# Recurrence of a hybrid block on Trainium2: the second head's inverse factors on the opposite partition half, and a new order of the level products

## The chip, the cores and the metric

The kernel runs on one core of a Trainium2 chip. The metric is the device time in microseconds; before the change the median of three runs is 2850.46 us. Engines are called PE (TensorE), DVE (VectorE), ACT (ScalarE), POOL (GpSimd) and SP (SyncE, which issues DMAs here).

## The reference

Two layers over 1024 tokens of width 1024. The first layer mixes with eight RWKV-7 heads of 64 beside eight heads of dilated attention, the second with a Fourier transform; each is followed by a convolved GLU. The change touches only the RWKV recurrence, run once forward and once reversed:

```python
def step(state, inp):
    r_t, w_t, k_t, v_t, kk_t, a_t = inp
    sk = jnp.einsum('bhij,bhj->bhi', state, kk_t)
    state = (state * w_t[:, :, None, :]
             - sk[..., :, None] * (kk_t * a_t)[:, :, None, :]
             + v_t[..., :, None] * k_t[:, :, None, :])
    y = jnp.einsum('bhij,bhj->bhi', state, r_t)
    return state, y
```

The kernel computes it by chunks of 64 tokens. Inside a chunk the feedback of `sk` on later tokens is a 64x64 strictly lower triangular matrix for each head; one plus it has to be inverted. Everything is fp32.

## The kernel before, in words

`recurrence` (L1343) takes the 1024 tokens as 8 pairs (`NPAIR`) of two chunks. `g` is the direction (0 forward, 1 reversed), `m` the pair, `c` the chunk in it, `f` one of four pairs of heads (`KU`), `hh` the head in it; a unit `u = hh * KU + f` is one of eight (`UN`). An SBUF tile has 128 partitions: head `hh` of a head pair lies on partitions `head(hh)`, and things that belong to chunk `c` lie on the half `side(c)`, the other half being `other(c)`. So a 64x64 matrix uses a quarter of PE's array: its rows by the half of the inputs, its columns by the half of the output. Each fp32 product of the code stands in the profile as two MATMUL records with two weight loads.

For one pair PE does, for both directions in turn: `turn` (transposes), `scores` (products of the factors, 64x128), `lower` (the triangular matrix the other way round), `values`, then five levels (`LEVELS` = 2, 4, 8, 16, 32) that build the inverse by doubling, then `solve`, `carry` and four `step`s, the only part that hands state from chunk to chunk.

A level i makes three products for each unit and chunk: x (`level_x`, L1553) multiplies the scores `xn` by the inverse so far (X1 or T); DVE copies the result under a mask into XL (L1807). Then t (L1572) multiplies the transposed inverse (U1 or U) by XL, and DVE copies it into T (L1813, L1815); and u (L1581) gives the transposed inverse again, which ACT copies into U (L1668, L1670). The last level has no t. X1 and U1 are the start of the inverse and of its transpose: DVE copies X1 from the `lower` product (L1790) and U1 from the scores (L1797), under a mask of neighbouring pairs.

PE's order in a level is x for g = 0 and 1, then t and u for g = 0, then t and u for g = 1 (L1633 to L1637). All factors for the next pair are made beside this: on DVE one piece (`beside`, L1871) after the X copies and one after the T copies of a level, in the order scan (L1839), centre (L1845, L1847), shift (L1852), alphas (L1860 to L1864), nbetas (L1869), each for g = 0 and 1; on ACT `f_rates` after level 0 and `f_exps` after levels 1 and 2; on POOL `f_products` and `f_outputs`. SP loads the data for the pair after that once these are done (L1465 to L1471). Every engine works its own list in order, with semaphores between them. PSUM has eight banks, four for each direction (`bank(g, k)`): x goes to bank 3, t to bank 0, u to bank 1.

The lines are written out by hand; no planner orders them. After `recurrence` a barrier ends the stage.

Of the kernel before, what the change touches and what calls it, by code (L numbers as in the profile page):

```python
# [14 lines left out]
P = 128  # L15
# [1327 lines left out]
def recurrence(nc, z_d, vr_d, lw_d, aa_d, kk_d, tab, consts, ff, ysum, low, mix_out, bon_d, gate_d, yb_d, factors):  # L1343
# [9 lines left out]
    with ExitStack() as ctx:  # L1353
# [31 lines left out]
        vec, K_A = consts["vec"], 5  # L1385
        pb = s.ps("pb", [P, 8, 512])

        def sems(name):
# [58 lines left out]

        def narrow(g, k, b):
            return bank(g, k)[:, 0:UN * HC].rearrange("p (u q b) -> p u q b", u=UN, b=b)

# [37 lines left out]
        def _(pe):  # L1488
# [18 lines left out]
            def scores(g, m):  # L1507
                t = st[m % 2][g]
                for part in range(2):
                    pe.wait_ge(tok_c[g], 5 * m + (2 if part == 0 else 5))  # L1510
                    for f in (2 * part, 2 * part + 1):
                        for c in range(2):
                            for hh in range(2):
                                four = t[head(hh), f, 0:2 * P].rearrange("p (n t) -> p n t", t=CH)
                                alpha_rho = four[:, 1:3, :] if c == 0 else four[:, 0::3, :]
                                at = ((f % 2) * 2 + c) * P
                                out = bank(g, 2 * part + hh)[:, at:at + P].rearrange("p (n t) -> p n t", t=CH)
                                ins = mm(out, t[head(hh), f, (2 + c) * P:(3 + c) * P], alpha_rho, start=True, stop=True)
                    ins.then_inc(q_done[g], 1)

            def lower(g, m):
                t = st[m % 2][g]
                pe.wait_ge(q_c[g], 4 * m + 2)
                for f in range(KU):
                    for c in range(2):
                        for hh in range(2):
                            nbeta = t[head(hh), f, 2 * P + CH + c * CH:2 * P + CH + (c + 1) * CH]
                            ins = mm(bank(g, hh)[side(c), f * CH:(f + 1) * CH], t[head(hh), f, (1 - c) * CH:(2 - c) * CH], nbeta,
                                     start=True, stop=True)
                ins.then_inc(l_done[g], 1)  # L1530

            def values(g, m):
                pe.wait_ge(q_c[g], 4 * m + 4)
                pe.wait_ge(tok_c[g], 5 * m + 5)
                for u in range(UN):
                    hh, f = divmod(u, KU)
                    for c in range(2):
                        ins = mm(bank(g, 2)[side(c), u * CH:(u + 1) * CH], xn[g][other(c), hh, 2 * f + c, 0:CH], wv[g][other(c), c, u, :],
                                 start=True, stop=True)
                ins.then_inc(mv_done[g], 1)  # L1540

            def level_x(g, m, i):
                b = LEVELS[i]
                src = X1[g] if i == 0 else T[g]
                if i == 0:
                    pe.wait_ge(x1_c[g], 2 * m + 2)
                else:
                    pe.wait_ge(t_c[g], 4 * m + i)
                for u in range(UN):
                    hh, f = divmod(u, KU)  # L1550
                    for c in range(2):
                        out = bank(g, 3)[side(c), u * HC:(u + 1) * HC].rearrange("p (q b) -> p q b", b=b)
                        ins = mm(out, xn[g][side(c), hh, 2 * f + c, 0:CH], cols1(src[side(c), u, :], b, 0), start=True, stop=True)  # L1553
                ins.then_inc(x_done[g], 1)

            def level_tu(g, m, i):
                b = LEVELS[i]
                old = U1[g] if i == 0 else U[g]
                if i == 0:
                    pe.wait_ge(u1_c[g], 2 * m + 2)  # L1560
                else:
                    pe.wait_ge(u_c[g], NL * m + i)
                pe.wait_ge(x_c[g], NL * m + i + 1)
                if i < NL - 1:
                    for u in range(UN):
                        for c in range(2):
                            if i == 0:
                                out, x = bank(g, 0)[side(c), u * CH:(u + 1) * CH], XL[i][g][side(c), u, :]
                            else:
                                out = bank(g, 0)[side(c), u * HC:(u + 1) * HC].rearrange("p (q b) -> p q b", b=b)  # L1570
                                x = cols1(XL[i][g][side(c), u, :], b, 0)
                            ins = mm(out, old[side(c), u, :], x, start=True, stop=True)  # L1572
                    ins.then_inc(t_done[g], 1)
                for u in range(UN):
                    for c in range(2):
                        if i == 0:
                            out, y = bank(g, 1)[side(c), u * CH:(u + 1) * CH], old[side(c), u, :]
                        else:
                            out = bank(g, 1)[side(c), u * HC:(u + 1) * HC].rearrange("p (q b) -> p q b", b=b)
                            y = cols1(old[side(c), u, :], b, 1)  # L1580
                        ins = mm(out, XL[i][g][side(c), u, :], y, start=True, stop=True)  # L1581
                ins.then_inc(u_done[g], 1)

            def solve(g, m):
                pe.wait_ge(u_c[g], NL * m + NL)
                pe.wait_ge(mv_c[g], m + 1)
                for u in range(UN):
                    hh, f = divmod(u, KU)
                    for c in range(2):
                        ins = mm(bank(g, 2 + hh)[side(c), f * P:(f + 1) * P], U[g][side(c), u, :], rz[g][side(c), u, :],  # L1590
                                 start=True, stop=True)
                ins.then_inc(z_done[g], 1)
# [53 lines left out]
        def _(act):  # L1646
# [13 lines left out]
            def values(g, m):  # L1660
                act.wait_ge(mv_done[g], m + 1)
                A(rz[g][:, :, CH:2 * CH], bank(g, 2).rearrange("p (u e) -> p u e", u=UN), ACT.Copy).then_inc(mv_c[g], 1)

            def level_u(g, m, i):
                b = LEVELS[i]
                act.wait_ge(u_done[g], NL * m + i + 1)
                if i == 0:
                    A(U[g][:, :, :], bank(g, 1).rearrange("p (u e) -> p u e", u=UN), ACT.Copy).then_inc(u_c[g], 1)  # L1668
                else:
# [38 lines left out]
            for m in range(NPAIR):  # L1708
# [3 lines left out]
                for i in range(NL):  # L1712
                    for g in range(2):
                        level_u(g, m, i)
                    if m + 1 < NPAIR:
                        if i == 0:
# [48 lines left out]
        def _(dve):  # L1765
# [19 lines left out]
            def lower(g, m):  # L1785
# [3 lines left out]
                for hh in range(2):  # L1789
                    V.copy_predicated(X1[g][:, hh * KU:(hh + 1) * KU, :], pairs[:, 0:1, :].broadcast_to([P, KU, CH]),  # L1790
                                      bank(g, hh)[:, 0:KU * CH].rearrange("p (f n) -> p f n", f=KU)).then_inc(x1_c[g], 1)

            def upper(g, m):
                dve.wait_ge(q_c[g], 4 * m + 4)
                for c in range(2):
                    mask = pairs[side(c), 1:2, :].rearrange("p (a b) n -> p a b n", a=1).broadcast_to([CH, 2, KU, CH])
                    V.copy_predicated(units(U1[g][side(c), :, :]), mask, xn[g][side(c), :, c::2, 0:CH]).then_inc(u1_c[g], 1)  # L1797

            def level_x(g, m, i):
# [6 lines left out]
                mask = level[:, i, :].rearrange("p (u q b) -> p u q b", u=1, b=b).broadcast_to([P, UN, HC // b, b])  # L1806
                V.copy_predicated(cols(XL[i][g][:, :, :], b, 0), mask, narrow(g, 3, b)).then_inc(x_c[g], 1)  # L1807

            def level_t(g, m, i):
                b = LEVELS[i]  # L1810
                dve.wait_ge(t_done[g], (NL - 1) * m + i + 1)
                if i == 0:
                    V.tensor_copy(T[g][:, :, :], bank(g, 0).rearrange("p (u e) -> p u e", u=UN)).then_inc(t_c[g], 1)  # L1813
                else:
# [39 lines left out]
            def f_alphas(g, m):  # L1854
# [35 lines left out]
            for m in range(NPAIR):  # L1890
                beside(m, 0)
                for phase in (scores, lower, upper):
                    for g in range(2):
                        phase(g, m)
                for i in range(NL):
                    for g in range(2):
                        level_x(g, m, i)
                    beside(m, 2 * i + 1)
                    if i < NL - 1:
                        for g in range(2):  # L1900
                            level_t(g, m, i)
                        beside(m, 2 * i + 2)
                for g in range(2):
# [1691 lines left out]
```

## Time and profile before

| | |
|---|---|
| median of three runs | 2850.46 us (2849.05 to 2860.39) |
| profiled execution, span from first to last instruction | 2846.2 us |
| profiled execution, what lies around the span | the page gives no number |
| recurrence | from the first transposes at about 671 us to the last product at 1122.8 us |
| one pair | 54.1 to 56.5 us |
| busy in the second pair (54.14 us) | PE 51.0, DVE 31.7, ACT 22.1, POOL 11.3 us |

PE's matmuls are pipelined: a row of the time line shows from the start of its first record to the end of its last, and the next row may start before that end. The pace of a block is therefore read from start to start.

### The profile page before, as it was taken

How to read it: one execution, taken by the hardware profiler on the slowest of the kernel's cores; microseconds unless marked ns; L12 is line 12 of the kernel's file. 1: busy time of each engine (PE TensorE's matmuls, PEld its weight loads, DVE VectorE, ACT ScalarE, POOL GpSimd, SP SyncE). 2: the span in 40 equal slices, each digit the busy share in tenths (PEclk: the TensorE clock that was granted, in tenths of full speed). 3: DMA queues.
4: the chain of work that ended last, by engine and by line, in shares of the span. 5: the costliest groups of instructions: out<-in, count | busy, mean ns of one | idle time of the engine just before them, and what ended most of it. 6: DMA issues, size and time to landing. Idle time of an engine off the chain costs nothing. (4 is left out here: it accounts for less than half of the span.)

```text
span 2846.2 us, 54939 instructions
## 1 busy us (share of the span) xinstructions
PE 2625.7 (92%) x23187; PEld 2149.5 (76%) x23187; DVE 1603.8 (56%) x2296; ACT 1138.0 (40%) x1802; POOL 918.1 (32%) x625
## 2 busy tenths in 40 slices
PE   5998998896999999979999999997897999999998
PEld 5776556576989888758888888875776888888887
DVE  7775532457555544666555564455655555556445
ACT  4211342553344333344444444454434444444434
POOL 2302121104112210225877770000412777773000
PEclk9999999898999999989999999997998999999999
DMA  6676434602311220422222228543122222225654
GB/s 232 229 270 215 168 133 175 186 17 64 92 48 48 71 91 27 133 80 69 89 83 77 86 90 284 169 164 109 52 92 71 89 89 74 82 89 216 191 181 145
DMA packets 295928, 346.48 MB, mean 122 GB/s; under 512 B 28384, under 2 KB 224213, under 8 KB 295685
## 3 DMA queue, kind: packets, MB, share of 16 engines
q1 hardware_dynamic: 286044, 336.64, 36.6%
q10 hardware_dynamic: 9640, 6.33, 0.7%
q8 instruction: 185, 3.03, 0.4%
q14 instruction: 59, 0.48, 0.1%
HBM read 271.58 MB, written 71.34 MB: 120 GB/s over the span
## 5 line engine op out<-in xcount | busy, mean ns | idle before, releaser
L2847 POOL TENSOR_TENSOR cg_u_lo<-cg_u_raw,cg_u_hi 128x512 fp32r<-128x512 f32 x210 | 315.2, 1509 | 146.8 <-ACT cg_u_hi L2733 146.8
L131 PE MATMUL cg_ps<-m_hi,cg_u_hi 128*128 128x512 f32 x844 | 331.2, 392 | 26.0 <-DVE cg_u_lo L2922 21.7
L133 PE MATMUL cg_ps<-m_hi,cg_u_lo 128*128 128x512 f32 x844 | 330.0, 391 | 0.0
L132 PE MATMUL cg_ps<-m_lo,cg_u_hi 128*128 128x512 f32 x808 | 315.5, 390 | 0.0
L2733 ACT ACTIVATE cg_u_hi<-cg_u_raw 128x512 fp32r<-128x512 f32 x216 | 132.1, 629 | 380.5 <-PE cg_ps L133 229.8
L131 PEld LDWEIGHTS cg_ps<-m_hi,cg_u_hi 128*128 128x128 f32 x844 | 159.7, 189 | 61.1 <-DVE cg_u_lo L2922 22.5
L131 PE MATMUL cg_ps<-over_y_tx,cg_u_hi 128*128 128x512 f32 x480 | 186.7, 389 | 0.0
L132 PE MATMUL cg_ps<-over_y_tx,cg_u_hi 128*128 128x512 f32 x480 | 186.7, 389 | 0.0
L133 PE MATMUL cg_ps<-over_y_tx,cg_u_lo 128*128 128x512 f32 x480 | 186.7, 389 | 0.0
L133 PEld LDWEIGHTS cg_ps<-m_hi,cg_u_lo 128*128 128x128 f32 x844 | 159.5, 189 | 33.5
L2899 DVE SCALAR_TENSOR_TENSOR cg_z<-cg_ps,top_conv_f,cg_z 128x1023 f32<-128x1023 f32 x88 | 113.0, 1284 | 115.1 <-ACT cg_z L2757 115.1
L132 PEld LDWEIGHTS cg_ps<-m_lo,cg_u_hi 128*128 128x128 f32 x808 | 152.7, 189 | 31.8
L2847 POOL TENSOR_TENSOR cg_u_lo<-cg_u_s,cg_u_hi 128x512 fp32r<-128x512 f32 x80 | 103.7, 1296 | 63.5 <-ACT cg_u_hi L2733 63.5
L1745 POOL TENSOR_TENSOR rw_kd<-rw_kd,att_kx 128x512 f32<-128x512 f32 x16 | 24.7, 1543 | 280.1 <-ACT rw_kd L1690 280.1
L2902 DVE SCALAR_TENSOR_TENSOR cg_z<-cg_ps,top_conv_f,cg_z 128x1023 f32<-128x1023 f32 x88 | 112.9, 1283 | 3.1
L131 PE MATMUL za_ps<-h_hi,za_w_hi 128*128 128x512 f32 x256 | 103.7, 405 | 8.2 <-POOL za_w_lo L1029 8.2
L2757 ACT ACTIVATE cg_z<-cg_ps,top_conv_f 128x1024 f32<-128x1024 f32 x88 | 98.1, 1115 | 21.0 <-DVE cg_ps L2959 11.6
L132 PEld LDWEIGHTS cg_ps<-over_y_tx,cg_u_hi 128*128 128x128 f32 x480 | 90.1, 188 | 18.7
L133 PEld LDWEIGHTS cg_ps<-over_y_tx,cg_u_lo 128*128 128x128 f32 x480 | 90.1, 188 | 18.7
L131 PEld LDWEIGHTS cg_ps<-over_y_tx,cg_u_hi 128*128 128x128 f32 x480 | 90.1, 188 | 18.7
L131 PE MATMUL cg_ps<-over_f_d_hi,cg_a_hi 128*128 128x512 f32 x248 | 97.4, 393 | 6.3 <-DVE cg_a_lo L2918 6.3
L132 PE MATMUL za_ps<-h_lo,za_w_hi 128*128 128x512 f32 x256 | 100.9, 394 | 0.0
(475 smaller groups left out, 6515.2 us busy)
## 6 DMA issues: line engine op xcount, KB each, us to landing
cg_u_raw<-in_ffn_up SPq DMA_DIRECT2D x88, 512.0 KB, 5.1
cg_u_raw<-in_ffn_down SPq DMA_DIRECT2D x64, 512.0 KB, 4.7
qkv_mw<-in_ada_w SPq DMA_DIRECT2D x12, 2048.0 KB
over_f_d_raw<-in_ffn_down SPq DMA_DIRECT2D x48, 512.0 KB, 5.2
scr_act<-cg_z SPq DMA_DIRECT2D x44, 512.0 KB, 2.7
qkv_mw<-in_ada_w SPq DMA_DIRECT2D x8, 1024.0 KB, 11.4
next_w<-in_mix_in SPq DMA_DIRECT2D x16, 512.0 KB, 6.6
za_out<-in_ada_w SPq DMA_DIRECT2D x8, 1024.0 KB
```

Source lines behind the costliest of these rows:

```text
L131: nc.tensor.matmul(out, a_hi, b_hi, start=first, stop=False)
L132: nc.tensor.matmul(out, a_hi, b_lo, start=False, stop=False)
L133: return nc.tensor.matmul(out, a_lo, b_hi, start=False, stop=last)
L1745: TT_(kd[g][:, :, :], kd[g][:, :, :], kx[g][:, :, :], ALU.mult).then_inc(f_kd[g], 1)
L2733: A(u_hi[:, n % RING], source(g, i), ACT.Copy).then_inc(uhi_done, 1)
L2757: A(z[:, x, :], both(g, x), ACT.Copy, scale=conv_cols[:, 1, g + x * FT:g + x * FT + 1]).then_inc(mid_done, 1)
L2847: G.tensor_tensor(u_lo[:, n % RING], source(g, i), u_hi[:, n % RING].bitcast(F32), ALU.subtract).then_inc(ulo_done, 1)
L2899: V.scalar_tensor_tensor(z[:, x, 1:S], both(g, x)[:, 0:S - 1], conv_cols[:, 0, c:c + 1], z[:, x, 1:S], ALU.mult, ALU.add).then_inc(left_do ...
L2902: V.scalar_tensor_tensor(z[:, x, 0:S - 1], both(g, x)[:, 1:S], conv_cols[:, 2, c:c + 1], z[:, x, 0:S - 1], ALU.mult, ALU.add).then_inc(con ...
```

## The change

1. For the second head (`u >= KU`) the start of the inverse and all that follows lie on `home(c, u) = other(c)`. `lower` writes the second head's U1 product as well, by 8 more products for each direction (16 records), and DVE copies that part of U1 from PSUM (one more copy for each direction), the first head's part still from the scores (64x256 instead of 64x512).
2. The factor alpha is stored with its halves in another order for the second head, so its write on DVE becomes two writes of 64 partitions each.
3. Products and copies of `values`, x, t, u and `solve` take `home(c, u)` for the second head. x, t, `values` and `solve` go over f, then hh, then c. Results of a level are spread over two banks: x and t in banks 0 and 1, u in banks 2 and 3, at 128 columns a unit.
4. Order of the levels on PE: x(0) for both directions, then for each level and direction t, u and directly behind them the x of the next level of the same direction. On DVE: T copy, one `beside` piece, next X copy, for each direction. On ACT `f_rates` and `f_exps` follow the U copy of their own direction, in levels 0 and 1.

The core of the diff:

```diff
-        def alpha_of(g, m):
-            a = halves(st[m % 2][g][:, :, 0:P])
-            return a[:, :, ::-1, :] if g == 0 else a[:, :, :, ::-1]
+        def alpha_of(g, m, hh):
+            a = halves(st[m % 2][g][head(hh), :, 0:P])
+            a = a if g == 0 else a[:, :, :, ::-1]
+            return a[:, :, ::-1, :] if g == hh else a
+        def alpha_slot(c, hh):
+            return slice(((1 - c) ^ hh) * CH, (((1 - c) ^ hh) + 1) * CH)
+        def home(c, u):
+            return side(c) if u < KU else other(c)
+        def wide(g, r):
+            return pw[:, (2 * g + r) * UN:(2 * g + r + 1) * UN, :]
@@ PE, lower
+                for f in range(KU):
+                    for c in range(2):
+                        nbeta = t[head(1), f, 2 * P + CH + c * CH:2 * P + CH + (c + 1) * CH]
+                        ins = mm(bank(g, 1)[other(c), (KU + f) * CH:(KU + f + 1) * CH], nbeta, t[head(1), f, alpha_slot(c, 1)],
+                                 start=True, stop=True)
@@ PE, level_x
-                for u in range(UN):
-                    hh, f = divmod(u, KU)
-                    for c in range(2):
-                        out = bank(g, 3)[side(c), u * HC:(u + 1) * HC].rearrange("p (q b) -> p q b", b=b)
-                        ins = mm(out, xn[g][side(c), hh, 2 * f + c, 0:CH], cols1(src[side(c), u, :], b, 0), start=True, stop=True)
+                for f in range(KU):
+                    for hh in range(2):
+                        u = hh * KU + f
+                        for c in range(2):
+                            out = wide(g, 0)[home(c, u), u, 0:HC].rearrange("p (q b) -> p q b", b=b)
+                            ins = mm(out, xn[g][side(c), hh, 2 * f + c, 0:CH], cols1(src[side(c), u, :], b, 0), start=True, stop=True)
@@ PE, level_tu: t (the same loops over f, hh, c), then u (still over u, c)
+                                    out = wide(g, 0)[side(c), u, 0:HC].rearrange("p (q b) -> p q b", b=b)
+                                    x = cols1(XL[i][g][home(c, u), u, :], b, 0)
+                                ins = mm(out, old[home(c, u), u, :], x, start=True, stop=True)
...
+                            out = wide(g, 1)[home(c, u), u, 0:HC].rearrange("p (q b) -> p q b", b=b)
+                            y = cols1(old[home(c, u), u, :], b, 1)
+                        ins = mm(out, XL[i][g][home(c, u), u, :], y, start=True, stop=True)
@@ PE, solve (the same loops over f, hh, c)
+                            ins = mm(bank(g, 2 + hh)[side(c), f * P:(f + 1) * P], U[g][home(c, u), u, :], rz[g][home(c, u), u, :],
+                                     start=True, stop=True)
@@ PE, order
+                for g in range(2):
+                    level_x(g, m, 0)
                 for i in range(NL):
                     for g in range(2):
-                        level_x(g, m, i)
-                    for g in range(2):
                         level_tu(g, m, i)
+                        if i + 1 < NL:
+                            level_x(g, m, i + 1)
@@ ACT, order
                 for i in range(NL):
                     for g in range(2):
                         level_u(g, m, i)
-                    if m + 1 < NPAIR:
-                        if i == 0:
-                            for g in range(2):
+                        if m + 1 < NPAIR:
+                            if i == 0:
                                 f_rates(g, m + 1)
-                        elif i <= 2:
-                            f_exps(i - 1, m + 1)
+                            elif i == 1:
+                                f_exps(g, m + 1)
@@ DVE, lower, upper, f_alphas
+                V.copy_predicated(U1[g][:, KU:UN, :], pairs[:, 1:2, :].broadcast_to([P, KU, CH]),
+                                  bank(g, 1)[:, KU * CH:UN * CH].rearrange("p (f n) -> p f n", f=KU)).then_inc(x1_c[g], 1)
...
-                    V.copy_predicated(units(U1[g][side(c), :, :]), mask, xn[g][side(c), :, c::2, 0:CH]).then_inc(u1_c[g], 1)
+                    V.copy_predicated(U1[g][side(c), 0:KU, :], pairs[side(c), 1:2, :].broadcast_to([CH, KU, CH]),
+                                      xn[g][side(c), 0, c::2, 0:CH]).then_inc(u1_c[g], 1)
...
-                V.tensor_tensor(alpha_of(g, m), halves(kk[g][:, :, :]), halves(lw[g][:, :, :]), ALU.mult).then_inc(f_alpha[g], 1)
+                V.tensor_tensor(alpha_of(g, m, 0), halves(kk[g][head(0), :, :]), halves(lw[g][head(0), :, :]), ALU.mult)
+                V.tensor_tensor(alpha_of(g, m, 1), halves(kk[g][head(1), :, :]), halves(lw[g][head(1), :, :]), ALU.mult).then_inc(f_alpha[g], 1)
@@ DVE, order
-                for i in range(NL):
+                for g in range(2):
+                    level_x(g, m, 0)
+                beside(m, 1)
+                for i in range(NL - 1):
                     for g in range(2):
-                        level_x(g, m, i)
-                    beside(m, 2 * i + 1)
-                    if i < NL - 1:
-                        for g in range(2):
-                            level_t(g, m, i)
-                        beside(m, 2 * i + 2)
+                        level_t(g, m, i)
+                        beside(m, 2 * i + 2 + g)
+                        level_x(g, m, i + 1)
```

## Rows read from the trace of the kernel before

**Rows 1.** The page, part 1: busy time, share of the span and instructions of each engine.

```profile
PE 2625.7 (92%) x23187; PEld 2149.5 (76%) x23187; DVE 1603.8 (56%) x2296; ACT 1138.0 (40%) x1802; POOL 918.1 (32%) x625
```

**Rows 2.** Windows, two chunk pairs: stretch, length, busy of five engines (instructions), clock, DMA, GB/s.

```profile
730.86:785.00 54.14, 51.01 (x1509) 49.56 (x1505) 31.72 (x60) 22.11 (x48) 11.27 (x8) 1.00 0.23 62
...
840.34:896.80 56.46, 52.66 (x1509) 51.21 (x1505) 31.57 (x60) 22.11 (x48) 11.25 (x8) 0.97 0.22 59
```

**Rows 3.** Time line of PE, second pair: start, duration, operation, records, [idle before].

```profile
739.44 0.69 PE L1528 MATMUL rw_pb<-lt_low 64*64 64x64 f32 x32 [0.48 <-DVE rw_xn L1781]
739.96 1.87 PE L1538 MATMUL rw_pb<-rw_wv,rw_xn 64*64 64x64 f32 x58
...
745.72 1.15 PE L1572 MATMUL rw_pb<-rw_XL,rw_U 64*64 64x64 f32 x32 [2.05 <-DVE rw_XL L1807]
746.67 1.13 PE L1581 MATMUL rw_pb<-rw_U,rw_XL 64*64 64x64 f32 x32
747.61 1.13 PE L1572 MATMUL rw_pb<-rw_XL,rw_U 64*64 64x64 f32 x32
...
749.47 2.04 PE L1553 MATMUL rw_pb<-rw_T,rw_xn 64*64 64x32 f32 x64
...
769.98 3.39 PE L1590 MATMUL rw_pb<-rw_rz,rw_U 64*64 64x128 f32 x58
...
773.49 2.00 PE L1599 MATMUL rw_pb<-rw_xn,rw_zt 64*64 64x128 f32 x60
776.08 0.69 PE L1612 MATMUL rw_pb<-rw_wv,rw_xn 128*64 128x64 f32 x16 [0.59 <-DVE rw_rg L1822]
```

**Rows 4.** Groups by line, DVE, fifth pair: count, busy us, mean ns, idle before.

```profile
L1807 DVE COPY_PREDICATED rw_XL<-rw_level,rw_pb 128x256 f32<-128x256 uint32 x10 | 4.8, 498 | 4.3 <-PE rw_pb L1553 4.3
L1797 DVE COPY_PREDICATED rw_U<-rw_pairs,rw_xn 64x512 f32<-64x512 uint32 x4 | 2.9, 731 | 0.1
L1815 DVE COPY rw_T<-rw_pb 128x256 f32<-128x256 f32 x6 | 2.5, 418 | 1.7 <-PE rw_pb L1572 1.6
L1839 DVE TENSOR_TENSOR_SCAN rw_cc<-rw_reset_row,att_lw 128x512 f32<-128x512 f32 x2 | 2.4, 1196 | 0.0
L1847 DVE TENSOR_TENSOR rw_cc<-rw_cc,rw_mids 128x512 f32<-128x512 f32 x2 | 2.3, 1168 | 0.1
L1852 DVE TENSOR_TENSOR att_lw<-rw_cc,att_lw 128x512 f32<-128x512 f32 x2 | 1.5, 772 | 0.0
...
L1790 DVE COPY_PREDICATED rw_X<-rw_pairs,rw_pb 128x256 f32<-128x256 uint32 x4 | 1.4, 436 | 0.0
L1862 DVE COPY rw_ends<-rw_e 128x4 f32<-128x4 f32 x2 | 1.4, 696 | 0.0
...
L1864 DVE TENSOR_TENSOR lt_low<-att_kk,att_lw 128x512 f32<-128x512 f32 x2 | 1.4, 678 | 0.0
```

**Rows 5.** Time line of DVE, second pair.

```profile
744.88 1.28 DVE L1807 COPY_PREDICATED rw_XL<-rw_level,rw_pb 128x256 f32<-128x256 uint32 x2
...
752.09 1.65 DVE L1847 TENSOR_TENSOR rw_cc<-rw_cc,rw_mids 128x512 f32<-128x512 f32 x1
```

**Rows 6.** Time line of ACT, second pair.

```profile
771.99 0.60 ACT L1675 ACTIVATE rw_zt<-rw_pb 128x512 f32<-128x512 f32 x1 [1.39 <-PE rw_pb L1590]
```

**Rows 7.** Windows, PE alone: stretch, length, busy (records), granted clock, DMA share, GB/s.

```profile
687.50:692.50 5.00, 3.84 (x79) 0.67 0.02 3
...
911.67:914.85 3.18, 3.18 (x64) 0.55 0.00 0
1023.50:1028.50 5.00, 4.40 (x103) 0.66 0.01 3
...
775.00:777.50 2.50, 1.91 (x62) 1.00 1.08 271
```

**Rows 8.** Time line of SP's queue, second pair: issue of the loads.

```profile
766.64 0.36 SPq L1471 DMA_DIRECT2D att_lw<-scr_lw  x1
```

**Rows 9.** Windows, PE alone, as rows 7: end of the loads' traffic.

```profile
777.50:780.00 2.50, 2.49 (x73) 1.00 0.71 197
```

More of the change, by code:

```diff
@@ L1514, in scores @@
                                 four = t[head(hh), f, 0:2 * P].rearrange("p (n t) -> p n t", t=CH)
-                                alpha_rho = four[:, 1:3, :] if c == 0 else four[:, 0::3, :]
+                                alpha_rho = (four[:, 1 - hh:3:1 + hh, :] if c == 0 else four[:, hh::3 - hh, :])
                                 at = ((f % 2) * 2 + c) * P
@@ L1534, in values @@
                 pe.wait_ge(tok_c[g], 5 * m + 5)
-                for u in range(UN):
-                    hh, f = divmod(u, KU)
-                    for c in range(2):
-                        ins = mm(bank(g, 2)[side(c), u * CH:(u + 1) * CH], xn[g][other(c), hh, 2 * f + c, 0:CH], wv[g][other(c), c, u, :],
-                                 start=True, stop=True)
+                for f in range(KU):
+                    for hh in range(2):
+                        u = hh * KU + f
+                        for c in range(2):
+                            ins = mm(bank(g, 2 + hh)[home(c, u), f * CH:(f + 1) * CH], xn[g][other(c), hh, 2 * f + c, 0:CH],
+                                     wv[g][other(c), c, u, :], start=True, stop=True)
                 ins.then_inc(mv_done[g], 1)
@@ L1564, in level_tu @@
                 if i < NL - 1:
-                    for u in range(UN):
-                        for c in range(2):
-                            if i == 0:
[L1568 to L1572, printed above, removed]
+                    for f in range(KU):
+                        for hh in range(2):
+                            u = hh * KU + f
+                            for c in range(2):
+                                if i == 0:
+                                    out, x = wide(g, 0)[side(c), u, 0:CH], XL[i][g][home(c, u), u, :]
+                                else:
+                                    out = wide(g, 0)[side(c), u, 0:HC].rearrange("p (q b) -> p q b", b=b)
+                                    x = cols1(XL[i][g][home(c, u), u, :], b, 0)
+                                ins = mm(out, old[home(c, u), u, :], x, start=True, stop=True)
                     ins.then_inc(t_done[g], 1)
@@ L1586, in solve @@
                 pe.wait_ge(mv_c[g], m + 1)
[L1587 to L1591, printed above, removed]
+                for f in range(KU):
+                    for hh in range(2):
+                        u = hh * KU + f
+                        for c in range(2):
+                            ins = mm(bank(g, 2 + hh)[side(c), f * P:(f + 1) * P], U[g][home(c, u), u, :], rz[g][home(c, u), u, :],
+                                     start=True, stop=True)
                 ins.then_inc(z_done[g], 1)
@@ L1661, in values @@
                 act.wait_ge(mv_done[g], m + 1)
[L1662 removed]
+                both_banks = pb[:, 4 * g + 2:4 * g + 4, 0:KU * CH].rearrange("p h (f e) -> p h f e", f=KU)
+                A(units(rz[g][:, :, CH:2 * CH]), both_banks, ACT.Copy).then_inc(mv_c[g], 1)
             def level_u(g, m, i):
@@ L1667, in level_u @@
                 if i == 0:
-                    A(U[g][:, :, :], bank(g, 1).rearrange("p (u e) -> p u e", u=UN), ACT.Copy).then_inc(u_c[g], 1)
+                    A(U[g][:, :, :], wide(g, 1)[:, :, 0:CH], ACT.Copy).then_inc(u_c[g], 1)
                 else:
```

29 lines of the change are left out of this document (14 added, 15 removed).

## The prediction

> **What bounds the kernel now.** Read first the busy line of the page: PE is busy 92% of the 2846.2 us span, the next engine, DVE, 56% [rows 1]. The page's chain of waits covers only the last quarter of the span, in other functions, so it says nothing of this stage; what a change here is worth must be read from the stage itself, which is one stretch of the time line: everything after it starts when its last product is out. The windows cut it into its eight chunk pairs, 54.1 to 56.5 us each [rows 2]. In the undisturbed second pair PE is busy 51.0 of 54.1 us, DVE 31.7, ACT 22.1, POOL 11.3. So PE bounds it, with one hole: before the first inverse product t0 it waits 2.05 us for DVE [rows 3]. I write x, t and u for the three products of a level and X, T, U for the copies that follow them on DVE, DVE and ACT.
>
> The time line of PE gives the price of a matmul record (one product of the code is two records). 64 records of x take 2.04 us of which the last one's tail is 0.2, 32 of t 0.95 from start to start (745.72 to 746.67), 32 of u 0.94: some 29 ns each, whether they stream 32 or 64 columns. They use two quarters of the array, since rows and output columns lie on the same half. `lower` already spreads over four quarters: 32 records from 739.44 to 739.96, 0.52 us or 16.3 ns each. With 128 columns, solve (two quarters) takes 3.5 us for 64 (769.98 to 773.49) and carry (four) 2.0 for 60, less a tail of 0.25, so 54 and 29 ns [rows 3].
>
> **The change on PE**, per pair, both directions. A block of 32 records going from two quarters to four falls from 0.93 to 0.52, by 0.41.
> - values: 2 blocks, -0.82. x: 10 blocks, -4.1. t: 8 blocks, -3.3. Solve: 3.5 to 1.9, -1.6.
> - u stays at 0.93: its rows and its output lie on the same half for either head.
> - `lower` gains 16 records a direction. They all read the second head's rows. Between 16.3 and 29.2 ns each that is 0.26 to 0.47; I take 0.47, +0.94, since they have only two quarters.
> - Scores, turn, carry and steps keep their counts.
> Together PE's work falls by 8.9 us a pair. That would be 71 us over eight pairs, if nothing else came late. DVE does.
>
> **Up to t0.** DVE sets this point today. After the scores it runs four X1 copies (0.44 each, 0.36 from start to start), four 64x512 U1 copies (0.73 each) [rows 4] and from 744.88 the first X (two of them 1.28, so 0.64) [rows 5]; then PE starts t0 at 745.72 [rows 3]. After the change: six copies of 0.36 instead of four (+0.72), and the U1 copies halve to 64x256. No row has that form; 0.73 of a form twice as long bounds it above and half of that, 0.37, below. I take 0.38, nearest to the 128x256 X1 copies at 0.36 each, so -1.4. The net is -0.7 a pair. The shorter values and x0 and the longer `lower` all lie before this point: the hole before t0 grows and they are worth nothing.
>
> **From t0 to solve**: today 745.72 to 769.98, 24.2 us without a hole [rows 3]. New PE work: t and x 8 blocks each at 0.52, u 10 at 0.93, together 17.6. Now the new order: for each direction t, u, and its next x directly behind them; on DVE T, one piece of the next pair's factors, then X. Half a level is 0.52+0.93+0.52 = 1.97 us of PE. DVE needs T 0.42 and X 0.44, from start to start 0.35 and 0.38, and the piece: centre 0.9 when alone (0.16 and 0.69) and up to 1.8 where it meets POOL (1.65 for its large part [rows 5], mean 1.17 [rows 4]), I take 1.4 for the second direction; shift 0.75; nbetas 0.65, like the product L1864 at 0.68; alphas that product and three small ones, one of which, a copy of 4 elements, has a mean of 0.70 where it meets POOL: 1.0 for the first direction and 1.8 for the second [rows 4]. The alphas are now two 64-partition writes: between 0 and another 0.6; I take 0.6, since the 64-partition form of 512 elements (0.73) is no cheaper than the 128-partition ones (0.68) [rows 4]. So:
> - The first T cannot start before the second X (0.64) and the scan (1.20) are through, and takes 0.62: some 2.5 us after the first X, where PE has work for 1.45. Hole 0.96.
> - The half level with the second direction's alphas: 0.35+2.4+0.38 = 3.13 against 1.97. Hole 1.16. The one before it (2.33) eats the slack, and centre (2.1 to 2.4) leaves 0.2 to 0.3 more; together some 0.35.
> Holes 2.5, stretch 20.1, saved 4.1. I followed the chain on the other side too: U must be copied before the same direction's next t, which is 2.5 us behind u, and ACT needs 0.2+0.38 plus at most one rates or exps piece of 1.6 to 1.8 before it. It just fits. POOL's pieces and the loads move with the factors: the loads for the next pair are issued from nbetas on (766.64) and their traffic lasts to about 780, 14 us [rows 8, 9]; the next scan starts some 17 us after nbetas, 3 us of cover (that cover gone, the scan and everything in DVE's queue behind it, the scores first, would be late).
>
> **From solve to the first step**: today 6.1 us (769.98 to 776.08). Solve and carry would be 1.9 and 1.9, but ACT is in between: a Z copy of 0.60 (771.99 [rows 6]), two wv copies of 0.6, then the other direction's Z copy; the second carry starts at about 3.7 instead of 4.4 and the first step, behind it on PE, at 4.65. Saved 1.4. Steps are as before.
>
> **Sum**: 0.7+4.1+1.4 = 6.2 us a pair for the seven pairs that carry factor work, 43.4; the last has none beside its levels, so no holes there: about 8.6. Total 52. From that I take 4: t and solve walk the halves in the order high, low, low, high, so neighbours share input rows, which `lower` and carry never do. Between 16.3 and 29.2 ns I take 19 for t, +0.8 of PE a pair, of which the holes hide some. Left: 48.
>
> One rule of the Trainium skill speaks against exactly this. "TensorE: Matmul & The Clock Gate", section "The mechanism" of its part on packing: a weight load overlaps matmuls in flight only when the row group differs. By it, t and solve would lose some of the gain; no row here has that order. The same page, "Wait — 56ns, not 53.3ns?", puts the least distance between matmul starts at about 25 ns. The 16.3 ns of `lower` contradicts it [rows 3]; by the page x and t would be 0.8 us a block and the time an estimated 2825.
>
> **Clock.** In four of eight pairs the granted clock fell from 2.4 to 1.2 GHz behind the hole before t0 (first and last row and the one at 911.67, with 3.18 us for what takes 1.87: 1.3 lost) [rows 7]. After the change the hole is longer (about 1.7, behind 0.8 in two parts), so I count a fall in all eight pairs. But t0 and u0 then run into the 0.96 in which PE would wait for T anyway, so each costs about 0.7: 5.6 against 5.2 today. Counted as nothing. A stretch that is 1.91 of 2.50 busy held 2.4 GHz [rows 7], and the levels will be about 85% busy.
>
> The profiled execution's span is 2846.2; 2846.2-48 = 2798, and the median of the runs lies 4.3 above the span, for what lies around it: **2803 us**.
>
> **Rivals.**
> 1. *Four quarters do not pay with these orders* (output in two banks, halves in another order; the change then does not do what it says). x, t, values, solve stay at 29 and 54 ns; what is left are the 0.7 before t0 and an equal loss in `lower` and the alphas. 2850, within 0.5%. For: no row has 64x32 on four quarters. Against: `lower` and carry hold 16 and 29 ns with either stride. Chance 0.08. In part (25 ns) it is 2825, inside the range.
> 2. *Slower: the clock stays at 1.2 GHz in the levels*, since they now have holes where today they have none. At 1.2 GHz a u block takes 1.73 instead of 0.93 (as t did at 911.67), x and t 0.96: half a level 3.65, the stretch about 32.7 against 20.1, +12.6. Against 6.2 gained, that is +6.4 a pair, 2901 if it always happens; it decides from about half of the stretch at the low clock. For: the falls at today's only hole. Against: 2.4 GHz at 76% busy. Chance 0.07.
> 3. *DVE holds less*: centre and alphas no longer meet POOL's writes (0.70 for a copy of 4 elements [rows 4], 1.65 for a centre of 0.69 [rows 5]), t at 16.3. Another 1.5 us a pair: 2791. Chance 0.15.
> 4. *DVE holds more*: pieces meet POOL in every half level, or PE stands more often for reasons that the profile does not name, as it does today in some pairs (the fourth is 2.3 us longer than the second [rows 2]). 2 us a pair: 2819. Chance 0.2.
> The forecast itself 0.5, its own range 2796 to 2810.
>
> 0.5% is 14 us, about what a measurement here can tell. Faster: forecast, rivals 3 and 4 and the partial case, 0.85; same 0.08; slower 0.07. The range goes from rival 3 to the partial case and a little of rival 1: 2788 to 2835.
>
> **What would show it.** Right: x and t blocks of 32 records at 0.5 to 0.6 us; u unchanged at 0.93; PE holes of about 1 us at x1 and x4, released by DVE's T; pairs of 47 to 49 us; solve to step 4.7. Wrong: blocks still at 0.9; t clearly slower than x; a granted clock of 0.5 inside the levels; a scan that waits for its load; PE waiting for ACT's U.

## The result, and the profile after

The changed kernel takes 2863.35 us (median of 20 runs, 2857.43 to 2869.55) against 2851.51 of before (20 runs). The ratio is 1.004, with a 95% interval of 1.0031 to 1.005: slower by 0.4%, where 1.7% faster was forecast. The profiled span is 2856.9 us against 2846.2.

The page's busy line of the changed kernel, beside [rows 1]:

```profile
PE 2610.3 (91%) x23443; PEld 2130.3 (75%) x23443; DVE 1627.2 (57%) x2328; ACT 1135.7 (40%) x1802; POOL 921.2 (32%) x625
```

PE has 15 us less to do and the span is 11 longer. The window of its second pair (stretch, length, busy of PE, PE's weight load, DVE, ACT and POOL with instructions, clock, DMA share, GB/s), beside [rows 2]:

```profile
732.80:790.20 57.40, 52.98 (x1541) 50.64 (x1537) 34.94 (x64) 21.85 (x48) 11.69 (x8) 0.79 0.21 59
```

57.4 us for 54.1, with a granted clock of 0.79 of full speed where it was 1.00. The time line of PE in the same pair, beside [rows 3]:

```profile
745.32 0.77 PE L1572 MATMUL rw_pb<-rw_X,rw_xn 64*64 64x32 f32 x36 [1.06 <-issue]
747.19 0.69 PE L1594 MATMUL rw_pb<-rw_XL,rw_U 64*64 64x64 f32 x32 [1.10 <-DVE rw_XL L1834]
747.67 1.61 PE L1603 MATMUL rw_pb<-rw_U,rw_XL 64*64 64x64 f32 x32
...
755.82 0.60 PE L1572 MATMUL rw_pb<-rw_T,rw_xn 64*64 64x32 f32 x28
...
756.29 0.65 PE L1594 MATMUL rw_pb<-rw_XL,rw_U 64*64 64x32 f32 x30
756.76 1.06 PE L1603 MATMUL rw_pb<-rw_U,rw_XL 64*64 64x32 f32 x30
...
764.59 1.08 PE L1572 MATMUL rw_pb<-rw_T,rw_xn 64*64 64x32 f32 x32 [0.55 <-DVE rw_T L1842]
765.46 1.06 PE L1594 MATMUL rw_pb<-rw_XL,rw_U 64*64 64x32 f32 x32
766.32 1.79 PE L1603 MATMUL rw_pb<-rw_U,rw_XL 64*64 64x32 f32 x30
...
775.70 3.46 PE L1613 MATMUL rw_pb<-rw_rz,rw_U 64*64 64x128 f32 x62
...
781.54 0.69 PE L1635 MATMUL rw_pb<-rw_wv,rw_xn 128*64 128x64 f32 x16 [0.34 <-DVE rw_rg L1849]
```

The reader is to see four things. The x block at 755.82 and the t block at 756.29 are 32 records each, a few of them in small rows that are left out here. With those, x goes from 755.74 to 756.23 and t from there to 756.76, where u follows: the four quarters do what was said, about 0.5 us a block. The u block is near the old 0.93 (756.76 to 757.69). But from 762 on the same blocks take twice as long: t from 765.46 to 766.32 is 0.86, and u from 766.32 on 1.5 and more. And solve starts 28.5 us after t0 (747.19 to 775.70), not 20.1 as forecast and not 24.2 as before. The windows of PE alone over the same stretch (busy with records, granted clock, DMA share, GB/s), beside [rows 7]:

```profile
747.19:755.00 7.81, 7.63 (x228) 0.56 0.02 4
755.00:762.00 7.00, 5.99 (x287) 0.98 0.02 7
762.00:775.70 13.70, 13.15 (x337) 0.50 0.48 138
775.70:781.50 5.80, 5.44 (x132) 0.73 0.53 136
```

The clock falls to 1.2 GHz behind the hole at t0, comes back near 755, and falls again at 762 behind a hole of 0.95 us in an x block (before 761.35, put down to "issue"). This time it stays down through all that is left of the levels, 13.7 us, although PE is 96% busy there (the wait of 0.55 before 764.59 lies inside this stretch). It comes back only in solve and carry. All eight pairs show such a long stretch, 10 to 17 us. Over the whole recurrence, before and then after:

```profile
680.00:1120.00 440.00, 407.79 (x11868) 0.98 0.20 58
```

```profile
680.00:1120.00 440.00, 386.00 (x11909) 0.84 0.21 60
```

A mean clock of 0.98 in 440 us is 18 us at 1.2 GHz, one of 0.84 is 141. And DVE meets POOL in new places; the alphas' two writes in this pair, where the kernel before has one write of 0.68 (L1864, [rows 4]):

```profile
761.39 0.67 DVE L1891 TENSOR_TENSOR rw_st<-att_kk,att_lw 64x512 f32<-64x512 f32 x1
762.08 1.67 DVE L1892 TENSOR_TENSOR rw_st<-att_kk,att_lw 64x512 f32<-64x512 f32 x1
```

### The profile page after: what moved, and what is told of

Its sections match the earlier page's. It is cut to its first block and busy times, and to the rows that moved or that the text cites. A ratio compares the mean times of both kernels' runs of the same rounds, so it can differ in the third digit from the quotient of the medians.

```text
span 2856.9 us, 55483 instructions
## 1 busy us (share of the span) xinstructions
PE 2610.3 (91%) x23443; PEld 2130.3 (75%) x23443; DVE 1627.2 (57%) x2328; ACT 1135.7 (40%) x1802; POOL 921.2 (32%) x625
## 5 line engine op out<-in xcount | busy, mean ns | idle before, releaser
L1603 PE MATMUL rw_pb<-rw_U,rw_XL 64*64 64x32 f32 (+1 forms) x2560 | 122.2, 258 | 4.7 <-issue 4.7
L1603 PEld LDWEIGHTS rw_pb<-rw_U,rw_XL 64*64 64x64 f32 x2560 | 115.6, 179 | 5.3 <-issue 5.3
```

The costliest lines, as they stand in the source:

```text
L1603: ins = mm(out, XL[i][g][home(c, u), u, :], y, start=True, stop=True)
```

## The experiments

Theory A when they began: the clock ate the gain; it falls behind holes of PE in the levels, and the 32-column blocks behind them do not bring it back. Its rivals were the order (B), holes alone with no part for the columns (C) and the four quarters themselves (D). The kernel before was run again in each set, with medians of 2848.27 to 2851.51; each ratio is taken to the one of its own set. A wait that the profile puts down to "issue" is one in which PE waited for nothing that the profile names.

**Taking the change apart.** The old order back in the changed kernel:

```diff
-                for g in range(2):
-                    level_x(g, m, 0)
                 for i in range(NL):
                     for g in range(2):
-                        level_tu(g, m, i)
-                        if i + 1 < NL:
-                            level_x(g, m, i + 1)
+                        level_x(g, m, i)
+                    for g in range(2):
+                        level_tu(g, m, i)
```

(the lists of ACT and DVE likewise)

> The changed kernel with the order of before (x of both directions, then t and u of each; DVE and ACT pieces where they were); halves and four quarters as changed. Theory A: the clock is what ate the gain. It falls behind a hole of PE in the levels and the 32-column blocks do not bring it back. PE is then as short of work as in the changed kernel, the holes are elsewhere, and the time stays near the changed kernel's: 2840 to 2870, with stretches at 1.2 GHz in most pairs. Rival B: the new order makes the holes, and four quarters alone would gain: 2800 to 2820, hardly a low clock in the levels.

Measured: 2857.97, ratio 1.0024 (1.0009 to 1.004); mean clock 0.84 in the recurrence, as in the changed kernel. B falls: it is not the order that loses the clock. The median is 5 us below the changed kernel's, with intervals that overlap, so a small price of the order is neither shown nor excluded.

The opposite, the new order alone in the kernel before (the three lists changed as in the diff of the change, no half moved):

> The kernel before with only the new order on PE, DVE and ACT; every product still on two quarters. Half a level is then 2.8 us of PE against at most 2.5 of DVE. Theory A: no holes in the levels, the clock holds, 2843 to 2855. Rival B (the order costs by itself): above 2860, with holes released by DVE's copies in the levels.

Measured: 2861.06, ratio 1.0036 (1.0019 to 1.0052), but its profiled execution is the shortest of the ten, 2847.84 (span 2846.1), with a clock of 0.99 in the recurrence. The median lies at the edge that B named and the profile where A expected it. The record has the mean clock of every execution over the whole kernel: 0.970 in the profiled one, 0.968 in the next shortest (2854.43), 0.958 to 0.963 in the other eight, 2857 to 2865. So part of the spread goes with the clock. It is not all: the kernel before has mostly 0.957 to 0.966 too, and a median 10 us lower. A cost of the order by itself, some 10 us here, stays open; the one profile does not show where it would lie.

**64 columns.** x, t and u stream all columns; the copies pick theirs:

```diff
-                            out = wide(g, 0)[home(c, u), u, 0:HC].rearrange("p (q b) -> p q b", b=b)
-                            ins = mm(out, xn[g][side(c), hh, 2 * f + c, 0:CH], cols1(src[side(c), u, :], b, 0), start=True, stop=True)
+                            out = wide(g, 0)[home(c, u), u, 0:CH]
+                            ins = mm(out, xn[g][side(c), hh, 2 * f + c, 0:CH], src[side(c), u, :], start=True, stop=True)
...
-            return wide(g, r)[:, :, 0:HC].rearrange("p u (q b) -> p u q b", b=b)
+            return cols(wide(g, r)[:, :, 0:CH], b, which)
```

> The changed kernel, but x, t and u stream all 64 columns in every level, and the copies pick the columns they need. The blocks are no longer at 2.4 GHz, since a record takes 16 and 29 ns with 32 and with 64 columns alike. Theory A says that the clock came back in before after 64-column blocks and does not after 32-column ones: here it falls as before in some places and comes back within 3 to 5 us, 2805 to 2835. Rival C: only holes matter, not columns: 2855 to 2870 as the changed kernel, low stretches of 15 us.

Measured: 2843.5, ratio 0.9965 (0.9951 to 0.9979), 20 us below the changed kernel for twice the columns. The mean clock is back to 0.95:

```profile
680.00:1120.00 440.00, 367.12 (x12276) 0.95 0.22 63
```

The low stretches in it last 3 to 7 us. C falls. The time is 8 us above A's range, though: the clock gave back 20 us, and something else holds.

**Less DVE work in the levels.**

```diff
+                k = KU if m < 2 else 1
-                V.tensor_tensor(lw[g][:, :, :], cc[g][:, :, :], lw[g][:, :, :], ALU.subtract).then_inc(f_before[g], 1)
+                V.tensor_tensor(lw[g][:, 0:k, :], cc[g][:, 0:k, :], lw[g][:, 0:k, :], ALU.subtract).then_inc(f_before[g], 1)
```

(alphas and nbetas likewise)

> The changed kernel with three quarters of DVE's shift, alphas and nbetas left out from the third pair on (it uses stale factors there). That takes away the hole at the alphas and leaves the one before t0. Theory A: with fewer holes the clock falls less often; levels from pair 3 on at 2.4 GHz past t0, 2800 to 2830. Rival D: the clock falls with 32-column blocks on four quarters whether there is a hole or not: 2850 or more.

Measured: 2859.36, ratio 1.0023 (1.0004 to 1.0041); mean clock 0.85. A's number fails. (This kernel leaves three quarters of the three pieces out from the third pair on and uses stale factors.) Seven of the eight pairs still lose the clock for 10 to 21 us. So the hole at the alphas is not needed: the clock also fell behind smaller ones, one of them behind a single "issue" wait of 0.98 us (fall at 883.1). The number is D's, but each of these falls has some wait of PE shortly before it, so D's "whether there is a hole or not" is not shown; no run has four quarters, 32 columns and no hole. The next two runs decide how far columns alone go.

**The same hole with 32 and with 64 columns, on two quarters.** In the kernel before, DVE gets extra work before the T copies of level 2 (`pad` is an unused tile, `padded` a new semaphore):

```diff
+                    if i == 2:
+                        for k in range(8):
+                            V.tensor_tensor(pad[:, :], reset_row[:, 0:416], reset_row[:, 0:416], ALU.mult).then_inc(padded, 1)
+                            dve.wait_ge(padded, m * 8 + k + 1)
```

> The kernel before with eight extra DVE operations (5 us) before the T copies of level 2, in every pair: a hole of PE of about 3 us in front of 32-column blocks on two quarters. The holes alone cost about 24 us: 2875. Theory A (32-column blocks do not bring the clock back): it falls in most pairs and stays at 1.2 GHz to the end of the levels, 12 us and more, 2900 to 2930. Rival C (the clock comes back after about 3 us whatever the blocks): 2875 to 2888.

> The same hole in the kernel before, but with 64 columns streamed in every level. Theory A: the clock falls as often and comes back within 3 to 5 us, 2875 to 2890, at least 15 below the run with the hole and 32 columns. Rival C: the same time as that run, within 5.

Measured: 2974.36 with 32 columns (four executions) and 2912.84 with 64 (three), ratios 1.0437 (1.0406 to 1.0468) and 1.0224 (1.0192 to 1.0255). A fourth execution with 64 took 7838.3 us; no run shows why, and it is left out. The holes came out as 6.8 us, not 3, so both lie higher than expected; the difference between them is some 61 us, 7.7 a pair. With 32 columns, the row behind the hole and windows of PE alone:

```profile
790.22 3.63 PE L1554 MATMUL rw_pb<-rw_T,rw_xn 64*64 64x32 f32 x64 [6.79 <-DVE rw_T L1816]
```

```profile
790.00:796.00 6.00, 5.78 (x108) 0.50 0.01 3
796.00:802.00 6.00, 6.00 (x118) 0.50 0.10 26
802.00:808.00 6.00, 6.00 (x112) 0.50 0.86 244
808.00:814.00 6.00, 6.00 (x108) 0.75 0.61 174
```

With 64:

```profile
788.53 3.68 PE L1554 MATMUL rw_pb<-rw_T,rw_xn 64*64 64x64 f32 x64 [6.80 <-DVE rw_T L1814]
```

```profile
790.00:796.00 6.00, 6.00 (x160) 0.72 0.01 3
796.00:802.00 6.00, 6.00 (x182) 1.00 0.66 188
```

With 32 columns the clock is still at 1.2 GHz in the window that ends at 808, with PE at work all the time since the hole, and comes back only in solve, which starts at 807.31. With 64 it is back some 5 us after the hole. Only the columns differ, and with them the places in PSUM that the copies read; no product is on four quarters. This shows the second half of theory A apart from the change.

The control, 64 columns in the kernel before without a hole (the diff of the 64-column run in the old layout):

> The kernel before with 64 columns in every level and nothing else. No hole in the levels and a record at 29 ns either way: 2845 to 2853, no change, by theory A too. If streaming the other 32 columns costs PE something that the start-to-start times hide, above 2860.

Measured: 2849.95, ratio 0.9989 (0.9973 to 1.0005). As expected, no change: where the clock does not fall, the columns are free and bring nothing.

**DVE's pieces out of the holes**, on the 64-column run:

```diff
                 beside(m, 0)
+                beside(m, 1)
...
-                beside(m, 1)
                 for i in range(NL - 1):
                     for g in range(2):
                         level_t(g, m, i)
-                        beside(m, 2 * i + 2 + g)
+                        if (i, g) in SLOTS:
+                            beside(m, SLOTS[i, g])
                         level_x(g, m, i + 1)
+                beside(m, 7)
...
+            SLOTS = {(0, 0): 2, (0, 1): 3, (1, 0): 4, (1, 1): 5, (2, 0): 8, (2, 1): 9, (3, 0): 6}
```

> The changed kernel with 64 columns in every level, and DVE's pieces moved out of the holes: the second scan before the scores, nbetas in level 2, the first direction's alphas in level 3, the second's behind the last X. If DVE's queue makes the holes at t0 and the alphas, PE's idle time in the levels falls by some 2 us a pair and with it the falls of the clock: 2815 to 2830. If the waits that the profile calls issue take over (27 us in the run with 64 columns, 7 before), it stays at 2832 to 2845. If the scans now wait for loads, above 2845.

Measured: 2830.55, ratio 0.9932 (0.9908 to 0.9956), between the two ranges. PE's waits for T in the levels went from 17.0 us in the 64-column run to 0.9 (680 to 1120), but its waits put down to "issue" grew to 45 us (before 7, changed kernel 13, 64 columns 27; these four from 735 to 1120). They have a pattern. Here is every row of PE's time line from one such wait to the next:

```profile
969.27 0.62 PE L1593 MATMUL rw_pb<-rw_XL,rw_U 64*64 64x64 f32 x25 [1.51 <-issue]
969.67 0.23 PE L1601 MATMUL rw_pb<-rw_U,rw_XL 64*64 64x64 f32 x2
969.72 0.22 PE L1593 MATMUL rw_pb<-rw_XL,rw_U 64*64 64x64 f32 x1
969.73 0.98 PE L1601 MATMUL rw_pb<-rw_U,rw_XL 64*64 64x64 f32 x28
970.50 0.27 PE L1572 MATMUL rw_pb<-rw_T,rw_xn 64*64 64x64 f32 x2
970.55 0.23 PE L1601 MATMUL rw_pb<-rw_U,rw_XL 64*64 64x64 f32 x2
970.61 0.63 PE L1572 MATMUL rw_pb<-rw_T,rw_xn 64*64 64x64 f32 x29
971.02 0.23 PE L1593 MATMUL rw_pb<-rw_XL,rw_U 64*64 64x64 f32 x1
971.02 0.22 PE L1572 MATMUL rw_pb<-rw_T,rw_xn 64*64 64x64 f32 x1
971.02 0.68 PE L1593 MATMUL rw_pb<-rw_XL,rw_U 64*64 64x64 f32 x31
971.54 0.33 PE L1601 MATMUL rw_pb<-rw_U,rw_XL 64*64 64x64 f32 x5
973.23 0.45 PE L1601 MATMUL rw_pb<-rw_U,rw_XL 64*64 64x64 f32 x9 [1.35 <-issue]
```

Count the records: 25+2+1+28+2+2+29+1+1+31+5 = 127, and the next piece starts with a wait of 1.35 us. In the levels of the other pairs such waits stand 126 to 128 records apart too, mostly 3.4 to 4.1 us, where solve begins up to 5.1. 127 records and as many weight loads are 254 instructions, 256 with two more. The Trainium skill, "Runtime: NRT & Kernel Launch", section "Instruction fetch mechanics", says that an engine's instructions are refilled in blocks of 16 KiB, 256 instructions, and that crossing a block is mostly hidden. The spacing agrees; that it is hidden does not hold here, with 45 us of waits. From this came theory S: PE's instructions arrive no faster than a block in about 3.6 us, and that bounds the levels. Two quarters at 29 ns use a block in 3.7.

The trace holds a more direct sign of it, since it records the transfers that bring instructions as well. From 735 to 1120 in the same run (queue, packets, MB, share of 16 engines):

```profile
q8 instruction: 84, 1.38, 1.5%
```

These are 84 transfers of 16384 bytes, one for some 128 of PE's 10774 records there, and each takes 0.9 to 1.4 us. Every one of the 44 "issue" waits ends 1.2 to 1.6 us behind the end of such a transfer; before the wait of 1.51 us at 969.27, for instance, one goes from 966.42 to 967.80. The same holds for all 8 of the kernel before and all 15 of the changed one (1.2 to 1.7 us). So these waits are waits for instructions, as far as times alone can show it. The next transfer starts 1.05 us or more after PE goes on, and two never start less than 3.3 us apart. A block thus costs a round trip, of which the transfer itself is the smaller part. The 3.6 us are the pace in the levels; in solve and the steps some waits stand 5 to 6.5 us apart, and what starts a transfer later there stays open.

**Array time or instructions.** u on four quarters too, records unchanged:

```diff
-                for u in range(UN):
-                    for c in range(2):
+                for f in range(KU):
+                    for hh in range(2):
+                        u = hh * KU + f
...
-                            out, y = wide(g, 1)[home(c, u), u, 0:CH], old[home(c, u), u, :]
+                            out, y = wide(g, 1)[side(c), u, 0:CH], old[home(c, u), u, :]
```

> On the run with 64 columns and DVE's pieces moved (2830.6): u is written to the half that makes it use all four quarters too, with the same number of records (the second head's inverse then stands on the wrong half, so this part is computed wrongly). It takes 10 blocks x 0.41 = 4.1 us a pair off PE. Theory S (PE's instructions arrive at one piece of 16 KB, 127 records with their loads, every 3.4 to 4.0 us, and that is now the bound): no change, 2822 to 2834. Rival P (products or holes bound it): 2797 to 2810.

And u without the last head pair in levels 1 to 4:

```diff
+                        if i and u % KU == KU - 1:
+                            continue
```

> The same 2830.6 kernel without the u products of the last head pair in levels 1 to 4 (left out, stale values stand there): 64 records fewer a pair, half a 16 KB piece. Theory S: 64/127 x 3.7 = 1.9 us a pair, 2812 to 2820. If DVE or the waits between engines bound it, nothing: 2826 to 2834. Together with the four-quarter u: less array time at equal records should bring nothing, fewer records should.

The first leaves the second head's inverse on the wrong half, the second leaves products out. Measured: 2832.05 (ratio 0.9943, 0.9926 to 0.996) with u on four quarters and 2818.83 (0.9891, 0.9872 to 0.991) with fewer records, against the 2830.55 (0.9932). The groups of u by line, of the run with the pieces moved and of the one with u on four quarters (count, busy us, mean ns, idle before):

```profile
L1601 PE MATMUL rw_pb<-rw_U,rw_XL 64*64 64x64 f32 x2240 | 84.4, 224 | 15.1 <-issue 15.0
```

```profile
L1600 PE MATMUL rw_pb<-rw_U,rw_XL 64*64 64x64 f32 x2240 | 54.3, 227 | 19.6 <-issue 18.7 <-DVE rw_XL L1831 0.9
```

30 us of u's array time went and not one came off the kernel; 64 records a pair less brought 12. Both numbers are those of S, and the rival of each fails. The profile of the first is less clean than its total: its levels are 8 us shorter over the eight pairs, and solve to the first step 6 us longer; waits for T came back (0.9 to 7.9 us from 735), and the clock is low for 48 us instead of 27. The pace agrees with S all the same. From t0 to solve a mean pair takes 24.1 us in the 2830.55 kernel, 23.1 with u on four quarters and 21.5 with 64 records less, which is 3.7, 3.5 and 3.6 us for each 127 records.

**The quarters under S.** The order and DVE's places of the 2830.55 kernel with 64 columns, all products on two quarters:

> The kernel before with 64 columns, the new order and DVE's pieces moved as in the 2830.6 kernel, but every product on two quarters as before. Its records at 29 ns are as fast as the pieces arrive (127 in 3.7 us). Theory S: the four quarters bring only what lies outside the levels and in buffered pieces, so this one comes to 2832 to 2845. Rival P: 2848 to 2855, the quarters being all of the gain.

Measured: 2851.02, ratio 1.0009 (0.9996 to 1.0021), with 4 us of "issue" waits. My number from S was wrong here and the range of its rival P holds: the quarters are worth 20 us, more than "29 ns is as fast as the blocks arrive" allows. The two profiles tell where. From the first transpose to the last pair's first step the 2830.55 kernel takes 426.3 us and this one 443.7. Of the 17.4, the levels give 12 (24.1 against 25.6 us from t0 to solve in a mean pair), the part up to t0 gives 5 and solve to the first step 3; the steps take 3 back. So two quarters do not reach the pace of the blocks in the levels, 3.9 us for 127 records against 3.7, with their one hole of 2 us already outside that stretch. S bounds the fastest versions; it does not make the quarters worthless.

**The hole before t0**, in the 2830.55 kernel:

```diff
-                for phase in (scores, lower, upper):
+                for phase in (scores, lower):
                     for g in range(2):
                         phase(g, m)
                 for g in range(2):
+                    upper(g, m)
                     level_x(g, m, 0)
```

> The same 2830.6 kernel, with DVE doing the first direction's U1 copies and first X before the second direction's U1 copies. The hole before t0 falls from 1.9 to about 1 us, with it some falls of the clock. If that hole and its falls still cost: 2818 to 2826. By theory S the pieces catch up in that hole and half of it is given back: 2824 to 2831.

Measured: 2827.14, ratio 0.9915 (0.9896 to 0.9933). The wait for the first X fell from 12.6 to 6.0 us in seven pairs. The time lies in the range of S and 1 us above the other one, and the two ratios have overlapping intervals, so the expectations are not told apart. It is the fastest version that computes everything, 0.85% below before.

## Why the prediction was wrong, step by step

- **Price of a block**: right. x and t at 0.47 to 0.52, u at 0.93, solve (1.8 in the 2830.55 kernel) as forecast. The neighbours that share input rows cost nothing visible: t is as fast as x, so the 4 us taken off for it were not needed, and the Trainium skill's rule on row groups ("TensorE: Matmul & The Clock Gate", "The mechanism") does not show here. The least distance of 25 ns between matmul starts that the same page of the Trainium skill gives ("Wait — 56ns, not 53.3ns?") does not hold either: 32 records in 0.5 us are 16 ns.
- **Up to t0**: -0.7 forecast, -0.5 measured (14.4 us from the first transpose to t0 against 14.9). Right.
- **Clock: the step that failed.** I wrote "Counted as nothing". The fall behind the longer hole was foreseen, but I priced it by the 3.2 us of a row in before, where 64-column blocks of level 0 follow the hole. The new holes stand in front of 32-column blocks, and there it lasts 10 to 17 us, to solve or beyond. The row that reassured me, 1.91 of 2.50 busy at full clock, is from the end of carry and the first step, with 128 and 64 columns [rows 7]; it says nothing of 32. 141 us at 1.2 GHz against 18 are some 120 us in which PE's blocks take double, 60 us of lost time at most, against the 48 forecast as gain. That is an upper bound: in the 64-column run the clock was mostly back and only 20 us came with it, since the next two terms then held. The fall is rival 2, which had 0.07 and a price of +6.4 a pair when it holds for the whole stretch; it held for about half of it, the break-even that I had worked out. That the time came out just above break-even is partly luck, as the other misses below are in it too.
- **Holes**: 2.5 us a pair forecast. In an undisturbed pair of the 64-column run (t0 at 916.99, solve at 941.14, 24.15 us) DVE's holes are 3.1. Mis-sized by a little: the second direction's shift and the first direction's alphas ran beside POOL's work as well (1.6 to 1.7 for 0.7), as in the rows above. Moving the pieces (2843.5 to 2830.55) was worth 13 us.
- **What was missing altogether**: the supply of instructions. Even at full clock the stretch is 24.15 us, not 20.1, as long as before the change; 3.1 of it are DVE's holes, 2.2 are "issue" waits, and some 1.2 beyond the 17.6 of work no wait explains. With DVE's holes gone the waits grow to take their place. Rival 4 named unexplained stops and took 2 us a pair for them together with DVE; it named no mechanism, and the before trace had one to find, since the two waits at 964.9 and 970.5 stand 127 records apart. Its example, the fourth pair, is mostly something else: 1.7 of its 2.3 us are a fall of the clock, 0.7 such a wait. And the pairs are not 54.1 to 56.5 us each, as I read: the windows left out the seventh, 59.3 us (1009.22 to 1068.50), and cut the sixth short (57.2). The two longest "issue" waits of that trace lie there, 1.7 us at 996.2 and 1.8 at 1064.4.
- **Solve to step**: 4.65 forecast, 5.84 measured in the changed kernel at the low clock (775.70 to 781.54), 5.05 at full clock in one pair of the 2830.55 kernel (986.48 to 991.53). The eight pairs of that kernel lie between 4.6 and 7.8; the long ones hold "issue" waits in solve. So this term was mis-sized too, by up to 1.2 us in the pairs shown.

## What to carry to other kernels

A stage in which PE is always busy can hide two limits that its neighbours only just meet: here DVE at up to 2.5 of PE's 2.8 us in half a level, and the instruction blocks at 3.6 of 3.7 us. Before halving the time of short matmuls, divide the records by 127 and ask whether PE would use up a block faster than in about 3.6 us. And where a faster PE will have holes, look at what stands behind each hole: the price of a clock fall is how long the blocks after it stay slow, so read it from a row with the same kind of block; where a run shows that streaming more columns costs no time, stream them.

## What the runs showed of the hardware

- Behind a hole of 6.8 us the granted clock stayed at 1.2 GHz through 17 us of gapless products with 32 columns and into solve, and for about 5 us when they had 64 columns, though at full clock a record takes 29 ns with either.
- A record of a 64x64x64 fp32 product (there are two of them) takes 29 ns on two quarters and 16 on four, the same with 32 columns; 30 us less array time at equal instructions changed nothing, 64 records less of some 1536 in each pair gained 12 us in all.
- PE stood still once every 126 to 128 records, for 0.2 to 1.9 us, when it used them in less than about 3.6 us; every such wait ended 1.2 to 1.6 us behind the end of a 16 KB transfer on the instruction queue, and these never started less than 3.3 us apart (2830.55 kernel).
